# Turning x before its norm is known, behind the first block of a two-block transformer kernel

## The reference

```python
def rmsnorm(x, g):          # rms_norm(x, g) is the same
    xf = x.astype(jnp.float32)
    y = xf * lax.rsqrt(jnp.mean(xf * xf, axis=-1, keepdims=True) + EPS)
    return (y * g.astype(jnp.float32)).astype(x.dtype)

def first_block(...):
    ...
    x = x + mod[:, 5, None] * swiglu(h2, w_up[l], w_down[l])
    return rmsnorm(x, g_final)

def swiglu_2(x, w_in, w_out):
    gate, up = jnp.split(x @ w_in, 2, axis=-1)
    return (jax.nn.silu(gate) * up) @ w_out

def second_block(x, ...):
    for i in range(DEPTH_2):
        g = norm_g[i]
        f = swiglu_2(rms_norm(x, g[0]), ffn_w_in[i, 0], ffn_w_out[i, 0])
        x = x + FFN_RESIDUAL_WEIGHT * rms_norm(f, g[1])
        ...
    return x
```

## Time and profile before

| what | value |
|---|---|
| median of 3 runs | 1449.38 us (1449.26 to 1451.11) |
| profiled execution, its time | 1450.4 us |
| profiled execution, its span | 1449.2 us |
| TensorE busy | 1420.4 us, 98% of the span |
| VectorE busy | 862.1 us, 59% |
| ScalarE busy | 763.8 us, 53% |
| granted TensorE clock, mean | 0.999 |

### The profile page before, as it was taken

The page is one execution under the profiler, slowest core; times in us unless marked ns, Lnnn a source line. Parts: engine busy times, 40 slices in busy tenths (PEclk is TensorE's granted clock), DMA queues, the critical chain, the costliest instruction groups (busy, mean ns, idle before and its releaser), DMA issues.

```text
span 1449.2 us, 19623 instructions
## 1 busy us (share of the span) xinstructions
PE 1420.4 (98%) x8042; PEld 1194.3 (82%) x8042; DVE 862.1 (59%) x1213; ACT 763.8 (53%) x1118; POOL 37.1 (3%) x72
## 2 busy tenths in 40 slices
PE   6999999999999999999999999999999999999998
PEld 5899889978888788888997888888888889888886
DVE  3628766875554765546576655557555475765543
ACT  4635355555444654446685655546444476754542
POOL 0000000000000000000241000000000000000000
PEclk9999999999999999999999999999999999999999
DMA  9537666555555655555534555565555551355552
GB/s 386 200 129 275 229 235 216 175 174 185 181 186 191 200 185 183 186 189 197 181 117 145 178 180 184 189 196 191 183 186 189 181 187 62 128 184 185 187 189 87
DMA packets 70075, 268.39 MB, mean 185 GB/s; under 512 B 7777, under 2 KB 8033, under 8 KB 66401
## 3 DMA queue, kind: packets, MB, share of 16 engines
q1 hardware_dynamic: 67968, 261.23, 53.5%
q10 hardware_dynamic: 2016, 5.90, 1.4%
HBM read 266.05 MB, written 1.05 MB: 184 GB/s over the span
## 4 chain that ended last, share of the span: by engine, by line
PE 92%; DVE 4%; ACT 2%; DMA 1%; issue 1%; SPq 0%; POOL 0%; ACTq 0%
PE PS L725 25%; PE PS L741 14%; PE PS L743 14%; PE PS L742 14%; PE PS L379 5%; PE PS L380 5%; PE PS L381 5%; PE PS L709 2%; PE PS L481 1%; PE PS L413 1%; DMA MC<-in_mod 1%; PE PS L414 1%; PE PS L415 1%; DVE WL L1667 1%; PE PS L1000 1%
## 5 line engine op out<-in xcount | busy, mean ns | idle before, releaser
L1667 DVE TENSOR_TENSOR WL<-RAW,WH 128x1024 fp32r<-128x1024 f32 (+1 forms) x440 | 534.0, 1224 | 283.4 <-ACT WH L1100 282.0
L1100 ACT ACTIVATE WH<-RAW 128x1024 fp32r<-128x1024 f32 (+1 forms) x440 | 452.2, 1054 | 263.3 <-DMA RAW<-in_up 134.7
L741 PE MATMUL PS<-WH,XH 128*128 128x512 f32 (+1 forms) x928 | 380.6, 410 | 4.7 <-DVE XL L2110 4.2
L743 PE MATMUL PS<-WH,XL 128*128 128x512 f32 (+1 forms) x928 | 362.1, 390 | 0.0
L742 PE MATMUL PS<-WL,XH 128*128 128x512 f32 (+1 forms) x928 | 361.7, 390 | 0.0
L741 PEld LDWEIGHTS PS<-WH,XH 128*128 128x128 f32 x928 | 174.3, 188 | 54.2 <-DVE XL L2110 8.0
L743 PEld LDWEIGHTS PS<-WH,XL 128*128 128x128 f32 x928 | 174.2, 188 | 37.2
L742 PEld LDWEIGHTS PS<-WL,XH 128*128 128x128 f32 x928 | 175.0, 189 | 27.7
L725 PE MATMUL PS<-WH,GH 128*128 128x512 f32 x440 | 137.7, 394 | 0.0
L725 PE MATMUL PS<-WL,GH 128*128 128x512 f32 x440 | 135.8, 390 | 0.0
L725 PE MATMUL PS<-WH,GL 128*128 128x512 f32 x440 | 135.6, 389 | 0.0
(11 more groups left out here) (350 smaller groups left out, 1832.5 us busy)
## 6 DMA issues: line engine op xcount, KB each, us to landing
RAW<-in_up SPq DMA_DIRECT2D x220, 512.0 KB, 3.6
RAW<-in_down SPq DMA_DIRECT2D x110, 512.0 KB, 3.3
RAW<-in_win SPq DMA_DIRECT2D x36, 512.0 KB, 4.6
RAW<-in_mod SPq DMA_DIRECT2D x16, 1024.0 KB, 6.6
MC<-in_mod SPq DMA_DIRECT2D x8, 1024.0 KB, 11.1
RAW<-in_sbqk SPq DMA_DIRECT2D x16, 512.0 KB, 5.0
GROW<-in_grow ACTq DMA_DIRECT2D x9, 512.0 KB, 5.3
RAW<-in_fg SPq DMA_DIRECT2D x8, 512.0 KB, 8.2
```

What stands on the lines that cost most here:

```text
L741: e.matmul(o_[:, 0:n], l, w[:, s], start=(k == 0), stop=False, skip_group_check=True)
L743: m = e.matmul(o_[:, 0:n], ll, w[:, s], start=False, stop=(k == KD - 1), skip_group_check=True)
L1100: e.activation(WH[s][:, 0:c], RAW[s][:, 0:c], ACT.Copy).then_inc(*sig("hi", j))
L1667: e.tensor_tensor(WL[s][:, 0:c], RAW[s][:, 0:c], WH[s][:, 0:c].bitcast(F32), ALU.subtract).then_inc(*sig("lo", j))
```

## The change

It touches boundary 1 alone, but for one small product.

- TensorE turns xa itself: `turn` waits for xa of that half in place of the renewed x. The turns of row block 0 come before the last two down steps of row block 1 and not behind them.
- VectorE's `updates` makes product and sum of one half before those of the other, n = 0 first. `scaled` multiplies with GFIN, the product of g_final and g[0] per feature (one instruction behind boundary 0).
- The renewal of x (with the reciprocal of the first norm and the row of g_final) is kept, since x itself is needed later, and stands behind the low parts of its row block. The number per row of the first norm is missing from the turned x, so the gates' scale RP is multiplied by it: one instruction of 128 x 1 more for each row block.
- ScalarE's instructions keep their order. Its square of xa waits for the half that is now added last.

```diff
--- before.py
+++ after.py
@@ -202,6 +202,8 @@
         VAC = VEC[:, 0:16].rearrange("p (k c) -> p k c", c=2)
         SSQ = [VEC[:, 16 + 4 * i:18 + 4 * i] for i in range(2)]
         RS = [VEC[:, 18 + 4 * i:20 + 4 * i] for i in range(2)]
+
+        GFIN = VEC[:, 24:32]
         EPS4 = VEC[:, 62:63]
         RAW2 = [at_(f"RAW2_{i}", [P, 2048], slot_at + 8192 * i) for i in range(SLOTS)]
 
@@ -693,7 +695,7 @@
 
                 o_, empty = bank(("xt", b, h, z), ("tn", b, h, z))
                 src = XN.of(("x", h)) if b == 0 else X[:, h, :]
-                pe.wait_ge(*at("x", b, h, z))
+                pe.wait_ge(*at("xa" if b == 1 else "x", b, h, z))
                 pe.wait_ge(*empty)
                 for y in range(4):
                     m = e.transpose(o_[:, y * P:(y + 1) * P], src[:, (4 * z + y) * P:(4 * z + y + 1) * P], IDN)
@@ -757,11 +759,11 @@
                     if ahead and p == n + LAG - 1:
                         ahead()
                     last = left is not None and p >= n + LAG - 2
-                    if last and left > 1:
+                    if last and left:
                         turn(left, 0, p - n - LAG + 2)
                     if p >= LAG:
                         step(p - LAG, 1)
-                    if last and left < 2:
+                    if last and not left:
                         turn(left, 0, p - n - LAG + 2)
 
             def out_step(name, kind, xh, xl, low, free):
@@ -1330,7 +1332,7 @@
 
                 sta = STA[:, 2 * b + h, :]
                 if b < 2 and n:
-                    ac.wait_ge(*at("xa", b, h, 0))
+                    ac.wait_ge(*at("xa", b, h, 1 if b else 0))
                     e.activation(JUNK[:, :], X[:, h, :], ACT.Square, accum_out=sta[:, 0:1]).then_inc(*sig("sq", b, h, 1))
                 elif b >= 2:
                     banks, end = block_end(b, h)
@@ -1379,10 +1381,10 @@
                 elif b < 7:
                     split(c0 + 4)
                     turned(b, 0, 0)
-                    if b > 1:
+                    if b:
                         turned(b, 0, 1)
                 square_of(b, 1, 0)
-                if b < 2:
+                if b == 0:
                     turned(b, 0, 1)
                 square_of(b, 1, 1)
                 root(b, 1)
@@ -2041,22 +2043,22 @@
                 dv.wait_ge(*come)
                 if b < 2:
                     dv.wait_ge(*at("mod", 12 * b + 11))
-                for n in (1, 0):
+                for n in (0, 1) if b == 1 else (1, 0):
                     y, before = Y.take(("y", b, h, n), ("xa" if b < 2 else "x", b, h, n))
                     dv.wait_ge(*after(before))
                     if b >= 2 and n == 0:
                         dv.wait_ge(*at("sq", b, h, 0))
                     e.tensor_tensor(y[:, :], BANK.of(banks[n])[:, :], grow[:, n * 512:(n + 1) * 512],
                                     ALU.mult).then_inc(*sig("y", b, h, n))
-
-            def added(b, h):
-
-                if b < 2:
-                    dv.wait_ge(s_x, 16)
-                    for n in (1, 0):
-                        x = X[:, h, n * 512:(n + 1) * 512]
-                        dv.wait_ge(*at("y", b, h, n))
-                        e.tensor_tensor(x, x, Y.of(("y", b, h, n))[:, :], ALU.add).then_inc(*sig("xa", b, h, n))
+                    if b == 1:
+                        added(b, h, n)
+
+            def added(b, h, n):
+
+                x = X[:, h, n * 512:(n + 1) * 512]
+                dv.wait_ge(s_x, 16)
+                dv.wait_ge(*at("y", b, h, n))
+                e.tensor_tensor(x, x, Y.of(("y", b, h, n))[:, :], ALU.add).then_inc(*sig("xa", b, h, n))
 
             def sum_of(b, h):
                 sta = STA[:, 2 * b + h, :]
@@ -2078,6 +2080,7 @@
                         XN.take(("x", h), None)
                     m = e.tensor_scalar(XN.of(("x", h))[:, c], x, r, None, ALU.mult)
                 elif b == 1:
+                    dv.wait_ge(*at("xt", b, h, n))
                     dv.wait_ge(s_grow[0], 32)
                     m = e.scalar_tensor_tensor(x, x, r, GROW[0][:, c], ALU.mult, ALU.mult)
                 else:
@@ -2098,8 +2101,10 @@
                         m = e.tensor_scalar(tn[:, c], BANK.of(("xt", b, h, z))[:, c], VEC[:, 40 + k:41 + k],
                                             MOD[:, 24 + k, 0:1], ALU.mult, ALU.add)
                 else:
-                    m = e.tensor_tensor(four(tn[:, :]), four(BANK.of(("xt", b, h, z))[:, :]),
-                                        bc(G2(*BEFORE[b], k0, 4), P), ALU.mult)
+                    if b == 1:
+                        dv.wait_ge(*at("dve", "gfin"))
+                    g = GFIN[:, k0:k0 + 4] if b == 1 else G2(*BEFORE[b], k0, 4)
+                    m = e.tensor_tensor(four(tn[:, :]), four(BANK.of(("xt", b, h, z))[:, :]), bc(g, P), ALU.mult)
                 m.then_inc(*sig("tn", b, h, z))
 
             def low_halves(b, h, q):
@@ -2116,7 +2121,12 @@
 
             def scale_of_input(b, h):
                 dv.wait_ge(*at("rq", b, h, "x"))
-                e.reciprocal(RP[:, b, h:h + 1], STA[:, 2 * b + h, 6:7]).then_inc(*sig("rr", b, h, "x"))
+                m = e.reciprocal(RP[:, b, h:h + 1], STA[:, 2 * b + h, 6:7])
+                if b == 1:
+                    m.then_inc(*sig("dve", "rr", h))
+                    dv.wait_ge(*at("dve", "rr", h))
+                    m = e.tensor_tensor(RP[:, b, h:h + 1], RP[:, b, h:h + 1], STA[:, 2 * b + h, 4:5], ALU.mult)
+                m.then_inc(*sig("rr", b, h, "x"))
 
             def scale_of_latents(h):
 
@@ -2125,11 +2135,41 @@
                     m = e.tensor_scalar(NRM[:, h, z:z + 1], RP[:, 5, h:h + 1], dim ** -0.5, None, ALU.mult)
                 m.then_inc(*sig("lat", h, "scale"))
 
+            def behind_first(c0):
+
+
+                updates(1, 0)
+                split(c0 + 3)
+                scaled(1, 0, 0)
+                inverse(1, 0)
+                scaled(1, 0, 1)
+                turned(1, 0, 0)
+                turned(1, 0, 1)
+                renewed(1, 0, 0)
+                renewed(1, 0, 1)
+                updates(1, 1)
+                split(c0 + 4)
+                scaled(1, 1, 0)
+                scaled(1, 1, 1)
+                turned(1, 1, 0)
+                scale_of_input(1, 0)
+                inverse(1, 1)
+                split(c0 + 5)
+                turned(1, 1, 1)
+                renewed(1, 1, 0)
+                renewed(1, 1, 1)
+                split(c0 + 6)
+                scale_of_input(1, 1)
+
             def boundary(b, c0, between=None):
+                if b == 1:
+                    return behind_first(c0)
                 updates(b, 0)
                 if b == 6:
                     between()
-                added(b, 0)
+                if b == 0:
+                    added(b, 0, 1)
+                    added(b, 0, 0)
                 if b < 2:
                     split(c0 + 3)
                 sum_of(b, 0)
@@ -2156,7 +2196,9 @@
                 updates(b, 1)
                 if b < 6:
                     turned(b, 0, 1)
-                added(b, 1)
+                if b == 0:
+                    added(b, 1, 1)
+                    added(b, 1, 0)
                 sum_of(b, 1)
                 if b < 7:
                     split(c0 + 4)
@@ -2168,8 +2210,6 @@
                         scaled(b, 1, 0)
                         split(c0 + 5)
                         turned(b, 1, 0)
-                        if b:
-                            scale_of_input(b, 0)
                         scaled(b, 1, 1)
                         turned(b, 1, 1)
                     else:
@@ -2250,6 +2290,7 @@
             for p in range(KD):
                 split(chunk["wo", 0] + p + AHEAD)
             boundary(0, chunk["up", 0])
+            e.tensor_tensor(GFIN, SM[:, S_GFIN:S_GFIN + 8], G2(*BEFORE[1], 0, 8), ALU.mult).then_inc(*sig("dve", "gfin"))
             ffn(0)
             boundary(1, chunk["up", UP])
             ffn(1)
```

## The result

The changed kernel takes 1452.69 us (median of 15 runs, 1452.44 to 1454.38) against 1449.26 us (15 runs, 1448.84 to 1451.11) for the kernel before. The ratio is 1.0023, 95% interval 1.0016 to 1.0030: slower by 3.4 us, a little over the 0.2% that was taken as the bound, which lies inside the interval. The forecast was 1452.6.

A forecast was written before the change was run, and what follows sets the result against it. TensorE was taken to bound the kernel (92% of the last-ending chain), so its added waits are paid in full. 0 + 1.00 + 2.22 = 3.2 us on the median 1449.38 gave 1452.6, range 1450.4 to 1455.2.

The forecast's parts named there:

- The queue before row block 1's sums: VectorE, boundary 1: row block 0's renewals ahead of row block 1's update make its sums end 1.00 us late.
- the renewals at the queue's end: VectorE, boundary 1: row block 1's renewals behind the low parts hold ScalarE's last square, adding 2.22 us.
- The chain of product and sum: VectorE's update: a sum needing the operation just before starts 0.73 us behind it, not 0.60; 2.74 us instead of 2.49.
- the forecast's lower bound: Whole kernel: 2.8 us slower instead of 3.2, if dependent operations cost no more than others.
- no gain on TensorE: Row block 0's turns, one down step earlier: same number, next block's first product still near 484.0, counted as 0.
- the second wait: TensorE before weight chunk c0+7's product: ready at 502.2, product at 504.26, so it waits 2.0 us.
- TensorE is ready at 502.2: Before chunk c0+7's product: from 494.47, five steps at 1.4 us and waits of 0.4 and 0.2.
- rival B: TensorE's clock falls in the new gaps of 2.6 and 2.0 us, giving 1455.2 us; chance 0.08.
- the sign that the forecast had given for B: TensorE's granted clock under 1.00 from 494 to 510 us in the changed kernel's profile.
- B's price of 2.6: Cost in us of a clock fall reaching beyond the waiting before 504.26: half of 5.3 us at half speed.
- Rival A: Boundary 1: the earlier turns carry through, three waits and 0.15 us vanish, 1447.9 us; chance 0.07.
- Rival C: ScalarE makes up time between 498 and 504, so only the high parts' +1.00 stays, 1450.4 us; chance 0.05.

The follow-up runs named there:

- e3: Changed kernel with row block 0's renewals behind row block 1's update and row block 1's in VectorE's pause before its low parts: 1449.19 us, ratio 0.9998 to before.
- e15: Changed kernel with product and sum of each half pulled apart again, as before the change: 1452.48 us, ratio 1.0018 to the kernel before.
- e14: Changed kernel with row block 0's turns behind their down steps again, as before the change: 1455.19 us, ratio 1.0039 to the kernel before.
- e5: Changed kernel with eleven overwritten products of row block 0 filling TensorE's gap before row block 1's first low part: 1453.78 us, ratio 1.0026 to before.
- e1: Changed kernel with only row block 0's two renewals of x moved behind row block 1's update on VectorE: 1452.42 us, ratio 1.0020 to before.
- e4: Changed kernel with weight chunk c0+7 split ahead of ScalarE's table load, the last square still late: 1451.57 us, ratio 1.0015 to before.
- e2: Changed kernel with only row block 1's reciprocal and two renewals moved into VectorE's pause before its low parts: 1451.70 us, ratio 1.0011 to before.
- e17: Changed kernel, row block 0's renewals behind row block 1's update, row block 1's between its turned halves, chunk c0+7 split early: 1449.36 us, ratio 0.9997 to before.

## Why the prediction was right, point by point

Distances from the first Y; forecast times of the prediction are set against 476.45, measured ones against 475.32.

| step | forecast | measured |
|---|---|---|
| row block 1's update starts | 486.14: 9.69 | 485.01: 9.69 |
| its last sum ends | 488.88: 12.43 | 487.74: 12.42 |
| TensorE at row block 1's turns, no wait | 489.6: 13.15 | 488.36: 13.04 |
| high parts of row block 1 | 493.56: 17.11 | 492.43: 17.11 |
| TensorE behind the low part, wait | 494.47: 18.02, 2.6 | 493.34: 18.02, 2.55 |
| last square | 498.20: 21.75 | 497.04: 21.72 |
| first product on chunk c0+7 | 504.26: 27.81 | 503.15: 27.83 |
| its wait | 2.0 | **0.98** |

- *The queue before row block 1's sums (+1.00) and the renewals at the queue's end (+2.22)* came as counted, to 0.03 us. Undone both, the loss is gone (e3).
- *The sum and the median*: 3.24 in D, 3.43 between the medians; the work behind the boundary is the same (948.05 and 948.16). The forecast left open on which side of 0.2% the result would lie, and so does the measured interval, 0.16% to 0.30%.
- *The chain of product and sum*: 0.25 per update, confirmed by e15, against the rule of the Trainium skill (page "VectorE: DVE Perf Modes", section "The DRAIN you can't avoid"). Of the 0.4 that the forecast's lower bound puts on dependent operations e15 takes away 0.30 in D; the rest was not tested.
- *The earlier turns, "no gain on TensorE"*: true as said, but it hid their worth. In the order that the change needs, they are worth 1.5 us (e14). The forecast had this in its path without naming it: 484.20 + 0.60 + 1.34 starts from turns at 480.33.
- *Mis-sized: the second wait*, 2.0 forecast and 0.98 measured. "TensorE is ready at 502.2" (25.75 from the first Y) was worked out at the full clock, and at the full clock it holds: in e5 TensorE comes to a stop at 25.90. In the changed kernel it is later, since rival B's mechanism was there: the clock fell in the first gap, to 0.50 between 494 and 496, which is the sign that the forecast had given for B. The prediction had said that such a fall would be swallowed for the most part, and it was, wholly (e5: D 27.80 with it taken away).
- *Rival B, beyond that*, gave it 0.08 that the fall costs anything. In the changed kernel it didn't. B's price of 2.6 was taken from 5.3 us of slow matmuls at the start, where the profile's granted clock reads 1.00; each fall that the clock's rows show took 1.70. But e1 and e5 show how near it was: there TensorE stood some 1.6 us ahead of c0+7 (0.20 and 1.36, 0.22 and 1.35), the clock fell behind it, and that was paid. In the changed kernel the first fall shortened the second wait to 0.98, behind which the clock stayed up. That it stayed up there in the profiled execution is luck. The forecast's reason against a fall was that 1.86 us had left the clock up in the fifth boundary, and behind that same wait it fell in four of the twelve profiled executions.
- *Rival A* falls: the high parts didn't move forward with the turns. *Rival C* falls too: c0+7 was the last to be late (e4).

## What to carry to other kernels

When an operation is made ready earlier, look at the queues of the engines behind it before counting on a gain: here the turns lost their wait, and all of it was lost again because ScalarE's high parts stood behind the same square and VectorE's renewals had been moved in front of one critical operation and behind another. Work that only has to be done some time belongs where its engine idles in any case, once it is known who waits for its result. Compare kernels by the distance between two events of the stage too: it shows differences of 0.3 us, which the medians can't tell. Then look at the rest of the span as well, because a fall of the clock behind the second event is in the time and not in the distance (e1, e5).

## What the hardware showed that was not expected

**The clock's fall is not set by the length of the wait ahead of it.** Behind waits of 2.54 to 2.56 us it fell in all four profiles (changed, e2, e4, e14), but not in two other executions of e2, whose mean granted clock is 1.000 (the length of their wait was not traced). Behind 2.31 us in e15 it did not, nor behind first waits of 1.2 to 1.4 us (e1, e3, e17). Behind 0.20 and 1.36 us with one small matmul between (e1), and 0.22 and 1.35 (e5), it fell; behind 0.22 and 1.35 in e15 it stayed at 1.00. And in the fifth boundary, which no run changes and where TensorE waits 1.85 or 1.86 us each time, it fell in four of the twelve profiled executions (e2, e4, e5, e15). There the stretches of e5 read, with 1.00 in both for the kernel before:

```profile
1170.00:1180.00 10.00, 8.14 (x44) 7.16 (x44) 9.70 (x20) 7.20 (x16) 0.00 (x0) 0.99 0.47 172
1180.00:1190.00 10.00, 9.94 (x56) 9.10 (x56) 6.84 (x20) 8.32 (x20) 0.00 (x0) 0.84 0.68 247
```

Each fall takes the same: 0.83 of the clock over ten microseconds, 1.7 us of progress. What the time shows of it goes by what waits behind: nothing in the changed kernel, and in the work behind the boundary 948.53 to 948.70 us with a fall in the fifth boundary alone (e2, e4, e15), where it is 947.80 to 948.16 with none behind D, 949.62 with one right behind D (e1) and 950.45 with both (e5). The Trainium skill (page "TensorE: Matmul & The Clock Gate", section "HAM oscillation — how this bites in real kernels") has the engine fall back when it idles and pay for the restart each time. That it falls and that it takes progress, these runs agree; that it does so each time, they don't: behind the fifth boundary's wait it stayed up in eight of twelve. What makes it fall behind 1.3 to 2.5 us in one execution and not in another stays open. A part of the spread between executions of one kernel comes with it (the groups of e1 and e2); how large a part in the other kernels was not measured.
